# VectorE's pass over a step's logits, in the step that makes them

## The reference

```python
for l in range(DEPTH):
    h = rmsnorm(x, norm_mix[l])
    proj = h @ w_in[l]
    (u, dq, dk, dv, iq, ik, iw, rq, rk, rv, rg) = jnp.split(proj, split_pts, axis=-1)
    y_a = s5_mixer(u, ...)
    y_b = dsa_attention(dq, dk, dv, iq, ik, iw, rel_bias)
    y_c = retention(rq, rk, rv, rg, ret_gn[l])
    x = x + jnp.concatenate([y_a, y_b, y_c], -1) @ w_out[l]
    gate, up = jnp.split(rmsnorm(x, norm_ffn[l]) @ w_ffn_in[l], 2, axis=-1)
    x = x + (jax.nn.silu(gate) * up) @ w_ffn_out[l]
```

```python
score = where(causal, einsum(relu(dots), w), NEG_INF)
_, sel = lax.top_k(score, 256)
logits = einsum(q, k[sel]) * scale + bias[t5_bucket(dist)]
p = softmax(where(dist >= 0, logits, NEG_INF)); out = einsum(p, v[sel])
```

## Time and profile before

| | us |
|---|---|
| median of 3 runs | 2772.22 (2771.98 to 2778.08) |
| profiled execution | 2779.92 |
| its span, first to last instruction | 2777.6 |
| TensorE busy | 2591.4 (93%) |
| VectorE busy | 1568.5 (56%) |
| GpSimd busy | 1312.8 (47%) |
| ScalarE busy | 1013.2 (36%) |

### The profile page before, as it was taken

One profiled execution on the slowest core, in us unless ns is written; L12 is line 12 of the kernel. 1 busy time (PEld: TensorE's weight loads), 2 busy tenths in 40 slices (PEclk: granted clock), 3 DMA queues, 4 the chain that ended last, 5 costly groups with the idle time before them and its releaser, 6 DMA issues. The chain is left out here.

```text
span 2777.6 us, 34714 instructions
## 1 busy us (share of the span) xinstructions
PE 2591.4 (93%) x13515; PEld 2035.0 (73%) x13515; DVE 1568.5 (56%) x2785; ACT 1013.2 (36%) x1472; POOL 1312.8 (47%) x818
## 2 busy tenths in 40 slices
PE   8798787989999999999999989989999999999998
PEld 6566655767777777778777767766777778888887
DVE  4859666778999224666232375477999942221111
ACT  5222144425343533323344422342434354322222
POOL 3332144435463475445555522443645356655655
PEclk9988899999999999999999999999999999999999
DMA  5232012222222144223222241221222224333332
GB/s 159 69 121 57 26 37 84 69 61 73 72 76 70 55 148 124 84 65 99 87 81 81 80 122 54 69 61 54 84 63 80 63 62 146 119 99 106 101 107 88
DMA packets 385665, 232.90 MB, mean 84 GB/s; under 512 B 29592, under 2 KB 371552, under 8 KB 383072
## 3 DMA queue, kind: packets, MB, share of 16 engines
q1 hardware_dynamic: 385136, 229.62, 27.9%
q10 hardware_dynamic: 368, 1.08, 0.1%
HBM read 213.88 MB, written 14.69 MB: 82 GB/s over the span
## 5 line engine op out<-in xcount | busy, mean ns | idle before, releaser
L681 POOL TENSOR_TENSOR w_lo<-w_raw,w_hi 128x1024 fp32r<-128x1024 f32 (+2 forms) x408 | 902.3, 2212 | 1322.4 <-ACT w_hi L792 1322.3
L1693 PE MATMUL psum<-h_hi,w_hi 128*128 128x512 f32 x1984 | 800.8, 404 | 17.4 <-ACT h_hi L816 7.1
L792 ACT ACTIVATE w_hi<-w_raw 128x1024 fp32r<-128x1024 f32 (+2 forms) x408 | 397.4, 974 | 1107.1 <-PE psum L1693 1070.9
L1693 PE MATMUL psum<-h_lo,w_hi 128*128 128x512 f32 x1984 | 770.1, 395 | 0.9 <-POOL h_lo L689 0.9
L1693 PE MATMUL psum<-h_hi,w_lo 128*128 128x512 f32 x1984 | 514.6, 390 | 0.0
L1693 PEld LDWEIGHTS psum<-h_hi,w_hi 128*128 128x128 f32 x1984 | 378.7, 191 | 130.1 <-issue 37.1
L1693 PEld LDWEIGHTS psum<-h_lo,w_hi 128*128 128x128 f32 x1984 | 378.2, 191 | 80.2 <-issue 1.9
L1693 PEld LDWEIGHTS psum<-h_hi,w_lo 128*128 128x128 f32 x1984 | 373.6, 188 | 76.7
L1313 DVE MAX8 top<-scores 128x8 f32<-128x512 f32 (+5 forms) x384 | 341.8, 890 | 8.1
L1315 DVE MATCH_REPLACE8 scores<-top,scores 128x512 f32<-128x512 f32 (+5 forms) x384 | 336.3, 876 | 0.0
L1693 PE MATMUL psum<-a_hi,w_hi 128*128 128x512 f32 x704 | 284.7, 404 | 18.3 <-DVE xs L1136 11.1
(11 more groups left out here) (296 smaller groups left out, 2945.4 us busy)
## 6 DMA issues: line engine op xcount, KB each, us to landing
w_raw<-in_w_ffn_in_dram SPq DMA_DIRECT2D x176, 512.0 KB, 3.8
w_raw<-in_w_ffn_out_dram SPq DMA_DIRECT2D x96, 384.0 KB, 3.1
w_raw<-in_w_in_dram SPq DMA_DIRECT2D x68, 512.0 KB, 3.8
w_raw<-in_w_out_dram SPq DMA_DIRECT2D x32, 512.0 KB, 3.6
x_half<-xs SPq DMA_DIRECT2D x8, 1024.0 KB, 6.8
xs<-x_half SPq DMA_DIRECT2D x8, 1024.0 KB, 6.9
w_raw<-in_w_ffn_out_dram SPq DMA_DIRECT2D x32, 256.0 KB, 2.6
out_dram<-mixed SPq DMA_DIRECT2D x8, 512.0 KB, 3.4
```

The source lines that it names most:

```text
L681: eng.tensor_tensor(w_lo(u, n), w_raw[:, u % 3, 0:n], w_hi[:, u % 2, 0:n].bitcast(F32), ALU.subtract).then_inc(sems["weights_ready"], 1)
L792: act(w_hi[:, u % 2, 0:n], w_raw[:, u % 3, 0:n], ACTF.Copy).then_inc(sems["hi_ready"], 1)
L1693: return eng.matmul(out_, lhsT, rhs, start=start, stop=stop, skip_group_check=True)
```

## The change

VectorE's pass moves from the step s=1 of a pair to its step s=0, behind `row_sums`. `block_out` stays in s=1. The rounds, the units' evictions and all other steps stay in their places of the plan; the other engines' programs are as before. Since the file is one line longer, line 1345 becomes 1348 and what follows in the file moves by one.

```diff
--- before.py
+++ after.py
@@ -1334,18 +1334,19 @@
             def attend(l, h, b, j, s):
                 at_, nk = attention[l, h], NK[b]
                 first = j == 0 and b == TT * h
-                if s == 0:
+                if s:
                     if j == 0 and not first:
-                        row_sums(at_)
+                        block_out(at_, b - 1)
                     return
+                if j == 0 and not first:
+                    row_sums(at_)
+
                 for n, g in enumerate(at_.banks):
                     i, c = 2 * j + n, "cd"[n % 2]
                     eng.wait_ge(sems[f"logits_{c}"], st.add(f"logits_{c}"))
                     eng.wait_ge(sems[f"mask{n % 2}_ready"], st.add(f"mask{n % 2}_ready"))
                     eng.tensor_tensor_reduce(bank(g, 0, nk), bank(g, 0, nk), at_.mask(b, n), -1.0, 3e38, ADD, ALU.min,
                                              nmax[:, i:i + 1]).then_inc(sems["nmax_ready"], 1)
-                if j == 0 and not first:
-                    block_out(at_, b - 1)
 
             def attend_end(l, h, s):
                 if s == 0:
```

## The result

| | before | after |
|---|---|---|
| median, us | 2775.15 (2771.98 to 2778.86) | 2858.74 (2857.34 to 2865.5) |
| profiled execution, us | 2779.92 | 2865.5 |
| its span, us | 2777.6 | 2863.4 |

The changed kernel takes 1.0304 times as long, 95% interval 1.0284 to 1.0324: 83.6 us slower. The forecast was 2861 us; for the profiled execution it was 2868.6, and that took 2865.5. (The runs of before were repeated beside those of after, which moved their median from 2772.2 to 2775.2.)

What follows compares the result with a forecast made beforehand. TensorE and VectorE, both almost full in the two late phases, were taken as the bound. 2 x (27.6 + 16) + 1.5 = 88.7 us on the median of 2772.2 gave 2861 us, range 2785 to 2888 (the forecast's own 2827 to 2878).

Steps and rivals of the forecast that it cites:

- The bound: Late phases, second-half attention woven between FFN units: TensorE and VectorE both almost full, 246.9 and 239.1 of 260 us.
- The loop: Late phases: VectorE waits for logits, TensorE's transposes for late evictions, in turn; 24.2 us longer per phase up to (7,0).
- Pass hidden behind ScalarE: Pairs whose last eviction is of a gate or up unit: SiLU and table load already cover the pass; moving gives nothing.
- The clock: Late phases: TensorE's granted clock falls behind eight stops, 2.0 us each, 16 us a phase, ends 0 and 22.
- Block 7: Last block of each late phase, without rounds: evictions come behind the pass, exponentials behind both; 3.4 us.
- The first half of layer 0: Block 2: two rounds come behind the pass of its first step, idle time pays half; +1.5 us, at most 3.
- The sum: Whole kernel: two late phases of 27.6 + 16 us plus 1.5 us, 88.7 us in all, giving 2861 us.
- The signs: Profile after: VectorE's idle time before the pass 81.1 to some 150 us, line 2013's waits 28.7 to about 75 us.
- (a): Late phases: stalls only replace VectorE's existing idle time; 0 to 12 us a phase, 2772 to 2796 us; chance 0.12.
- (b): Faster: transposes' waits go because nmax is ready before the units between the steps are done; 2735 us; chance 0.07.

Runs made afterwards that it cites:

- filler kernel: Changed kernel plus 24 unread transposes of a constant ahead of the real ones in seven of a late phase's eight long stops: 2847.76 us, ratio 1.0260.
- the kernel behind the last eviction: Against the kernel before, pass moved ahead of the rounds following the last of several evictions between a pair's steps: 2766.23 us, repeated 2767.67 us.

## Why the prediction was right, step by step

**The bound.** Right: both engines nearly full in the late phases, and all but some 8 us of the loss lies there.

**The loop.** Right in place and size. Logits of (4,0) to (7,0) took 36.4 and 36.2 us more. By block in the first phase it was 17.5, 10.3 and 8.6, block 4 most, as said; the down stretch, from (5,0)'s logits to those of (5,2), ran in 47.9 instead of 51.3 us, as said. The stops before transposes measured 3.89, 3.05, 3.69, 3.04 in block 4 (forecast 3.95, 3.0, 3.8, 2.95), 4.38 and 4.58 in (5,2) and (5,3) (4.5, 4.75), 3.71 and 3.87 in (6,0) and (6,3) (3.8, 5.5); only the last is off, and it is 2.26 us in the second phase. VectorE's stalls at the logits of (4,1), (4,2), (4,3), (5,0), (5,3), (6,0) and (6,1) were 5.6, 7.2, 5.4, 4.1, 7.6, 3.0 and 5.7 us, against the list of 3.5, 7.5, 4.6, 2.7, 7.8, 3.0 and 5.3. Without the clock the loop is worth 23.7 and 26.2 us by the filler kernel, against 24.2; by block in the first phase 11.8, 5.8 and 6.0 us, where the loop written down gives 12.9, 4.8 and 6.5.

**Pass hidden behind ScalarE.** Right for the changed kernel: in its blocks 4 to 6 the exponentials of the first phase never wait for `nmax`. For the kernel before it was said too widely. Where rounds stand between the last eviction and the pass, `nmax` came last there too, as in (4,2):

```profile
664.85 0.80 ACT L1011 ACTIVATE scratch<-psum,nmax 128x640 f32<-128x640 f32 x1 [2.80 <-DVE nmax L1345]
```

TensorE was still busy with its unit (its transposes at 667.16 have no stop), so moving the pass gave nothing there all the same. What counts for the stops is the time of the last eviction.

The exponential starts 1.30 us behind the load's start (659.48, 660.78 in the changed kernel). The page "ScalarE: Activation LUTs" of the Trainium skill, section "What ACT_TABLE_LOAD costs", adds a drain of about 1380 ns; the trace again has no room for it, and the stops came out at the sizes worked out without it.

**The clock.** Right in kind; the size is an average that scatters. 2.0 us a stop, 16 a phase, were forecast, all of it on the path. The filler kernel shows 14 and 13 us of slow busy time for its seven stops, 2.0 and 1.8 a stop, and 12.7 and 10.0 us of it reach the end. In the kernel with the change in second halves only the same stops cost 9 and 15.5. The forecast sat at the upper edge of this: up to (7,0) it gave 40.2 us a phase, and the four phases measured are 36.4, 36.2, 30.3 and 39.1 us longer.

**Block 7.** 3.4 forecast, 2.7 and 4.3 measured from (7,0)'s to (7,3)'s logits.

**The first half of layer 0.** Mis-sized: 1.5 forecast, at most 3, and 4.7 measured. I counted the rounds behind the pass but not `block_out` behind these rounds, whose bank TensorE needs, nor the clock behind that stop, which is half of the 4.7 us in this profile and absent in another (64.8 for 67.1 us). A step that stays put is delayed too when one is moved in front of what precedes it.

**The sum.** From the profiles, after less before: start of the first attention +2.1 (not of the change, below), from there to (4,0) of the first phase +6.2 (4.7 of it in the attention), the phases up to (7,3) +39.0 and +40.5, between them -0.8, behind -1.3: 85.8 with the rounding, the difference of the spans. Forecast: 43.6 twice and 1.5, 88.7. Each phase came out 3 to 5 us shorter than forecast, and the rest 4.8 longer, 2.1 of it not from the change. That the median lies 2.3 us from the forecast is partly luck: these misses have opposite signs, and the median of before, to which the 88.7 us were added, came out 3 us higher when it was measured again; the difference itself is 83.6 us.

**The signs.** The waits of line 2013 (now 2014) were to be about 75 us and are 69.4. VectorE's idle time before the pass was to be some 150 us and is 240.5, with 58.7 more put down to issue: in first halves and block 7 the wait for TensorE moved from evictions to the pass (line 1136 from 295.8 to 251.3, line 1276 from 280.0 to 200.5), which I had not counted. It costs far less than its length: the first halves cost some 8 us in all by the medians.

**The rivals.** (a), that VectorE's idle time pays, fell with the stretches: it had 26 us and would have needed 64. (b), faster, fell in gate and up stretches by the stops. In down stretches its mechanism exists (in (5,1) and (6,2)) but the pass in s=0 bought nothing alone: that kernel was slower. The kernel that is faster moves the pass by rounds, never past an eviction.

## What to carry to other kernels

Before moving a step ahead of its neighbours on one engine, ask two things of the trace: is its input there when the engine arrives in the new place, and who waits for each instruction that is now behind it. A result that is not the last to come can be computed late at no cost; an eviction that starts another engine's chain can't. Count idle time put down to issue among the waits. Move such a step up past work that nobody waits for (here search rounds), and stop behind the last result that somebody does.

## What the runs showed of the hardware

**Clock behind a stop.** Stops of nearly one length are followed by different clocks. The changed kernel's transposes of (4,1) and (4,3), ten each, stand behind stops of 3.05 and 3.04 us. The first took 2.37 us (at 661.81, above), the second 1.54, where behind a covered stop in the filler kernel ten take 1.51:

```profile
717.98 1.54 PE L2014 MATMUL psum<-cst,scratch 128*128 128x128 f32 x10 [3.04 <-ACT scratch L1011]
```

In the kernel with the change in second halves only it was the other way round: 1.51 us at (4,1), 2.37 at (4,3), behind stops of 3.04 us both. A price for each stop is an average. In the filler kernel the engine stood still for 0.4 to 2.0 us at those places, and the mean clock of the stretch was 0.99.

**A scatter ahead of the change.** The kernels differ before any instruction that an edit touched: the first attention's logits start between 359.8 and 366.2 us. One wait that shows it is TensorE's for VectorE's line 1378 at 150 us, in before and in the kernel with the change in first halves only:

```profile
150.47 1.97 PE L2040 MATMUL psum<-cst,scratch 128*128 128x128 f32 x16 [0.94 <-DVE scratch L1378]
```

```profile
152.01 3.67 PE L2040 MATMUL psum<-cst,scratch 128*128 128x128 f32 x16 [5.77 <-DVE scratch L1378]
```

The stop is 0.9 to 2.0 us in four of the profiles and 5.8 in eight, and the 16 transposes behind it take 272 ns each behind the short one and 421 behind the long one. Two profiles of one and the same program (the kernel behind the last eviction, twice) both had 5.8. Whether it belongs to the program or to the execution stays open, and it isn't all of the scatter: with 5.8 the attention starts anywhere from 362.3 to 366.2 us. The best kernel gains 8 to 10 us, so stretches of the trace measured from the same instruction say more here than spans do.
